# Blank TensorE products first, the first norm's weights through full-height products, and weight tile 1 ahead of token tile 2

## The reference, cut to what matters

```python
def rmsnorm(x, g):
    xf = x.astype(jnp.float32)
    y = xf * lax.rsqrt(jnp.mean(xf * xf, axis=-1, keepdims=True) + EPS)
    return (y * g.astype(jnp.float32)).astype(x.dtype)
...
        hn = rmsnorm(h, mix_pre[l])
...
    u = h @ w_in
    gate_br, x_br = u[..., :D_RNN], u[..., D_RNN:]
```

## Time and profile before

| | us |
|---|---|
| median of three runs | 1112.71 |
| lowest and highest | 1111.16, 1113.22 |
| the profiled execution's own time | 1111.33 |
| its span | 1109.5 |
| TensorE busy in it | 1093.1 |
| first real product starts | 11.77 |

### The profile page before, as it was taken

One profiled execution on the slowest core, in us unless ns is written; L12 is line 12 of the kernel. 1 busy time (PEld: TensorE's weight loads), 2 busy tenths in 40 slices (PEclk: granted clock), 3 DMA queues, 4 the chain that ended last, 5 costly groups with the idle time before them and its releaser, 6 DMA issues.

```text
span 1109.5 us, 17385 instructions
## 1 busy us (share of the span) xinstructions
PE 1093.1 (99%) x6901; PEld 977.4 (88%) x6901; DVE 780.9 (70%) x1117; ACT 557.0 (50%) x980; POOL 14.9 (1%) x34
## 2 busy tenths in 40 slices
PE   8999999999999999999999999999999999999998
PEld 7887787889899999988888888879899999998886
DVE  5788985778688888853347888558788888863334
ACT  6377474555355555532236576545355555542223
POOL 1000000000000000000020000000000000000000
PEclk9999999999999999999999999999999999999999
DMA  6332233234133323333333132122233333333211
GB/s 203 111 91 68 84 98 119 92 90 138 42 111 115 111 85 110 134 116 100 104 80 76 39 97 57 39 76 84 88 115 114 96 95 115 115 133 98 100 50 76
DMA packets 150962, 107.22 MB, mean 97 GB/s; under 512 B 23922, under 2 KB 140770, under 8 KB 150883
## 3 DMA queue, kind: packets, MB, share of 16 engines
q1 hardware_dynamic: 150882, 106.12, 31.7%
HBM read 104.01 MB, written 2.10 MB: 96 GB/s over the span
## 4 chain that ended last, share of the span: by engine, by line
PE 93%; DVE 4%; ACT 2%; DMA 1%; issue 0%; POOL 0%; SPq 0%; DVEq 0%
PE ps L1758 11%; PE ps L1760 11%; PE ps L1762 11%; PE ps L1536 10%; PE ps L1537 10%; PE ps L1540 10%; PE ps L1517 9%; PE ps L1518 8%; PE ps L1519 8%; PE ps L1689 1%; PE ps L1862 1%; PE ps L1889 1%; DVE w_lo L976 1%; DVE work L1166 1%; ACT junk L562 1%; DVE h L1168 1%
## 5 line engine op out<-in xcount | busy, mean ns | idle before, releaser
L976 DVE TENSOR_TENSOR w_lo<-raw,w_hi 128x1024 fp32r<-128x1024 f32 x113 | 140.4, 1245 | 166.5 <-ACT w_hi L558 166.3
L558 ACT CAST w_hi<-raw 128x1024 fp32r<-128x1024 f32 x114 | 118.9, 1046 | 168.9 <-PE ps L1540 147.5
L1517 PE MATMUL ps<-x_hi,w_hi 128*128 128x512 f32 (+1 forms) x520 | 180.8, 348 | 4.9 <-DVE w_lo L976 4.2
L1518 PE MATMUL ps<-x_lo,w_hi 128*128 128x512 f32 (+1 forms) x520 | 177.5, 341 | 0.0
L1519 PE MATMUL ps<-x_hi,w_lo 128*128 128x512 f32 (+1 forms) x520 | 177.4, 341 | 0.0
L1758 PE MATMUL ps<-t_hi,w_hi 128*128 128x256 f32 x576 | 163.5, 284 | 0.2
L1760 PE MATMUL ps<-t_lo,w_hi 128*128 128x256 f32 x576 | 163.4, 284 | 0.0
L1762 PE MATMUL ps<-t_hi,w_lo 128*128 128x256 f32 x576 | 163.4, 284 | 0.0
L1536 PE MATMUL ps<-w_hi,t_hi 128*128 128x512 f32 x352 | 137.3, 390 | 0.0
L1537 PE MATMUL ps<-w_lo,t_hi 128*128 128x512 f32 x352 | 137.3, 390 | 0.0
L1762 PE MATMUL ps<-x_hi,w_lo 128*128 128x256 f32 x432 | 122.5, 284 | 0.0
(11 more groups left out here) (202 smaller groups left out, 2011.0 us busy)
## 6 DMA issues: line engine op xcount, KB each, us to landing
raw<-in_ffn_w_gu SPq DMA_DIRECT2D x88, 512.0 KB, 4.0
raw<-in_ffn_w_down SPq DMA_DIRECT2D x44, 512.0 KB, 3.3
raw<-in_a_w_in SPq DMA_DIRECT2D x24, 512.0 KB, 4.3
raw<-in_a_w_out SPq DMA_DIRECT2D x12, 512.0 KB, 3.5
raw<-in_b_w_q SPq DMA_DIRECT2D x16, 256.0 KB, 3.4
raw<-in_b_w_o SPq DMA_DIRECT2D x16, 256.0 KB, 3.8
h<-in_x SPq DMA_DIRECT2D x4, 512.0 KB, 5.8
result<-h SPq DMA_DIRECT2D x3, 512.0 KB, 2.6
```

The lines of the kernel that those rows point to most:

```text
L558: nc.scalar.copy(w_hi[:, t % 4, :], raw[:, t % 4, :]).then_inc(w_hi_ready, 1)
L976: v.tensor_tensor(w_lo[:, t % 4, :], raw[:, t % 4, :], w_hi[:, t % 4, :].bitcast(F32), ALU.subtract)\
L1517: nc.tensor.matmul(out_ps, hi_w, hi_x, start=first, stop=False)
L1518: nc.tensor.matmul(out_ps, hi_w, lo_x, start=False, stop=False)
```

## The change

Five edits, all at the start of the kernel:

- VectorE first of all zeroes `gain_rows` (128 partitions by 1,024 float32) and `blank` (128 by 512 bf16) and fills `ones` (128 by 128 float32) with ones. GpSimd no longer fills the row of ones.
- SP loads x0 first, then waits until `gain_rows` is zeroed, and loads the row of weights into its first partition; the rest follows in the order of before.
- TensorE waits for the three fills, makes four bf16 products of 128 x 128 by 512 columns of zeros into PSUM bank 5, then spreads the weights by products of full height (the rows but the first are zero), and makes four more blank products.
- TensorE multiplies weight tile 1 with the first 256 tokens directly behind tile 0, and turns token tile 2 only then, followed by token tile 3.
- ScalarE splits weight tile 1 before it squares x2, and tile 2 before the high part of token tile 2; VectorE makes the low parts of tiles 1 and 2 one step earlier likewise.

```diff
--- before.py
+++ after.py
@@ -151,7 +151,6 @@
     ri_raw = sb("ri_raw", [P, 2, RI_COLS], F32, at["gpost"])
     junk = sb("junk", [P, D], BF16)
     ident = sb("ident", [P, P])
-    ones_row = sb("ones_row", [1, P])
     eps = sb("eps", [P, 1])
     ss = sb("ss", [P, 32])
     std = sb("std", [P, 33])
@@ -186,7 +185,9 @@
     r_rows = sb("r_rows", [P, P], F32, at["e_u"])
     dist_i = sb("dist_i", [P, WIN], I32, at["e_u"] + 4 * P)
     dist_n = sb("dist_n", [P, WIN], F32, at["e_u"] + 8 * P)
-    gain_row = sb("gain_row", [1, D], F32, at["y_lo"])
+    gain_rows = sb("gain_rows", [P, D], F32, at["y_lo"])
+    ones = sb("ones", [P, P], F32, at["y_lo"] + 4 * D)
+    blank = sb("blank", [P, S], BF16, at["y_hi"])
 
 
     at["top"] = U
@@ -286,6 +287,8 @@
         xhi_ready = sem("xhi_ready")
         xlo_ready = sem("xlo_ready")
         eps_ready = sem("eps_ready")
+        blank_ready = sem("blank_ready")
+        gain_blank = sem("gain_blank")
         xf_ready = sem("xf_ready")
         t_ready = sem("t_ready")
         thi_ready = sem("thi_ready")
@@ -433,8 +436,9 @@
             def load_x(c):
                 sp.dma_start(h[:, c, :], x[0, c * P:(c + 1) * P, :]).then_inc(x_landed[c], 16)
 
-            sp.dma_start(gain_row[:, :], mix_pre[0:1, :]).then_inc(gain_landed, 16)
             load_x(0)
+            sp.wait_ge(gain_blank, 1)
+            sp.dma_start(gain_rows[0:1, :], mix_pre[0:1, :]).then_inc(gain_landed, 16)
             load_x(1)
             load_in(0)
             load_x(2)
@@ -505,7 +509,6 @@
                 pool.wait_ge(pool_steps, steps.inc(ins))
 
             nc.gpsimd.memset(eps[:, :], EPS).then_inc(eps_ready, 1)
-            nc.gpsimd.memset(ones_row[:, :], 1.0)
             then(nc.gpsimd.memset(ident[:, :], 0.0))
             nc.gpsimd.affine_select(out=ident[:, :], in_=ident[:, :], compare_op=ALU.not_equal, fill=1.0, base=0,
                                     pattern=[[-1, P]], channel_multiplier=1).then_inc(ident_ready, 1)
@@ -588,11 +591,11 @@
             split_hi(0)
             for i in range(4):
                 first_high(i)
+            split_hi(1)
             square_x(2)
-            split_hi(1)
             square_x(3)
+            split_hi(2)
             first_high(4)
-            split_hi(2)
             first_high(5)
             act.wait_ge(lam_abs, 1)
             nc.scalar.activation(sp_t[:, 1, :], sp_t[:, 0, :], ACT.Exp, scale=-1.0).then_inc(lam_exp, 1)
@@ -1007,15 +1010,18 @@
                 v.tensor_tensor(x_lo[:, k0:k1, tok], turned_in(t)[:, k0:k1, :], x_hi[:, k0:k1, tok].bitcast(F32),
                                 ALU.subtract).then_inc(first_lo, 1)
 
+            v.memset(gain_rows[:, :], 0.0).then_inc(gain_blank, 1)
+            v.memset(blank[:, :], 0.0)
+            v.memset(ones[:, :], 1.0).then_inc(blank_ready, 1)
             for i in range(4):
                 normalise_x(i)
             for i in range(4):
                 first_low(i)
+            split_lo(1)
             normalise_x(4)
-            split_lo(1)
             normalise_x(5)
+            split_lo(2)
             first_low(4)
-            split_lo(2)
             first_low(5)
 
 
@@ -1629,12 +1635,20 @@
                     token_half(b, 2, t, 1)
 
 
+            def busy(n):
+
+                for _ in range(n):
+                    nc.tensor.matmul(bank(5), blank[:, 0:P], blank[:, :], start=True, stop=True)
+
+            pe.wait_ge(blank_ready, 1)
+            busy(4)
             pe.wait_ge(ident_ready, 1)
             pe.wait_ge(gain_landed, 16)
             for half in range(2):
-                ins = nc.tensor.matmul(bank(6 + half), ones_row[:, :], gain_row[:, half * S:half * S + S], start=True,
+                ins = nc.tensor.matmul(bank(6 + half), ones[:, :], gain_rows[:, half * S:half * S + S], start=True,
                                        stop=True)
             ins.then_inc(gain_spread, 1)
+            busy(4)
 
             def first_turn(i):
                 t, k0, k1 = START_PARTS[i]
@@ -1652,8 +1666,8 @@
             for i in range(4):
                 first_turn(i)
             first_half(0)
+            first_half(1)
             first_turn(4)
-            first_half(1)
             first_turn(5)
             first_half(2)
             pe.wait_ge(params_landed, 16 * 8)
```

## The result

Twenty runs of the changed kernel have a median of 1114.99 us (1112.52 to 1115.71); twenty of the kernel before, 1112.51 (1111.08 to 1114.17). The ratio is 1.0017, 95% interval 1.0011 to 1.0023: slower by about 2 us, clear of no change, and 1 us above the top of the range forecast. The profiled execution took 1115.27 us against 1111.33. Both kernels' runs lie in groups a microsecond or more apart: the lowest runs differ by 1.4 us, the medians by 2.5.

The account below looks back on a forecast made before the run. TensorE, busy 99%, bounds the kernel, so the first real product's start decides. +0.95 - 0.25 = +0.7 on the profiled 1111.33 gave 1112.0; half the spread, 0.4, made it 1112.4, range 1110.7 to 1114.0.

Parts of the forecast that it names:

- T0: Start of TensorE's first real product, 11.77 us before; forecast 12.7, a later start moving the whole rest of the kernel.
- (a): VectorE's three memsets ahead of everything: 1.9 us in all, blanks starting at 2.65, no cost to VectorE.
- (b): SP's queue: x0 0.41 us earlier, later loads behind a wait; tile 0 lands at 8.0, x1 at worst 7.0.
- the weight chain: Tile 0's load, ScalarE's rounding, GpSimd's low part, ending at 11.65 before; forecast to allow T0 likely at 11.6.
- (c) to (e): Gain row lands at 4.5, four blanks take 1.9 us, full-height gain products 3.1, ending at 7.6.
- (f): VectorE's first normalising product waits for the gain products until 7.6; with 5.12 us behind it, T0 12.7, +0.95.
- (g): The swap of tile 1's first half and token tile 2's turn: no turn waits afterwards, -0.25 us.
- The term that was put at nothing: TensorE's clock behind T0: already risen by then in the profiled run, so blanks can give back nothing there.
- half of the spread above the profiled run: Median over profiled execution: blanks take away what a late-rising clock causes, so only half stands, 0.4 us.
- the slower one (the row queues): SP's gain row lands at 6.6 behind x0, the clock stays low, T0 16.1, time 1115.4; chance 0.06.
- Rival 4: The swap stalls: tile 1 lands over a us after 12.15, its first half waits, 1113 us; chance 0.11.
- Rival 3: Blanks don't raise TensorE's clock: gain products take 3.75 us, T0 14.0, time 1113.3; chance 0.12.

Follow-up runs that it names:

- row_second: The kernel before with x0 loaded ahead of the row of weights, without a wait: lowest +2.2, median +2.0 us, ratio 1.0019.
- swap_only: The kernel before with only tile 1's first half put ahead of the turn of token tile 2: lowest -0.25, median +0.15 us, ratio 0.9996.
- act_queue: The changed kernel with the row of weights and its wait moved from SP's to ScalarE's queue: lowest +2.8, median +2.0 us, ratio 1.0025.
- row_waits: The kernel before with x0 ahead of the row and SP waiting between them on a VectorE memset: lowest +3.25, median +2.2 us, ratio 1.0023.
- wait_only: The kernel before, row still first, with SP waiting on a VectorE memset between x0 and x1: lowest +0.8, median +0.9 us, ratio 1.0009.
- two_fills: The kernel before with the swap and blanks only where TensorE idles, three behind the gain products, two behind the last turn: ratio 0.9991, again 0.9994.
- early_fill: The kernel `two_fills` with two more blanks ahead of the gain products: 1111.20 us against 1112.64 for the kernel before, ratio 0.9991.

## Why the prediction was wrong

The forecast was "about the same". The sum gave the start +0.7 us where the profiled execution lost 2.5: 0.3 of the difference lies in T0, 1.5 behind it. Point by point:

- (a) The memsets took 0.91, 0.27 and 0.17, less than the 1.9 in all; VectorE started at 1.01 and not at 0.73, so the blanks began at 2.40 for 2.65. Right.
- (b) **This is the step that failed** ahead of T0. It said that the loads queue for bandwidth anyway, that x1 lands at worst at 7.0 and tile 0 at worst at 8.85, likely 8.0. x1 came at 7.97, tile 0, 6.7 us behind its issue, at 9.41. The bounds took the time from issue to landing from one execution, in which SP never paused. For x1 the pause and the row make it longer: 4.4 to 4.7 us with the row first or on another queue, 5.3 with the wait, 5.4 with the row, 5.1 to 6.5 with both. For tile 0 the bound was too narrow even without them: it took 5.6 to 7.3 us in kernels with the row first and no pause. So both chains were late, the weight chain too, and T0 was 13.06 for 12.7.
- (c) to (e) Row at 4.66 for 4.5, blanks 1.89 for 1.9, gain products 2.94 for 3.1, their end 7.60 for 7.6: right here, near the lucky end of a term that gave 2.60 to 3.75 in other executions. In the other two profiles of this kernel it gave 3.75 and 3.70, so that the gain's own chain, and not x1, held T0 at 13.29 and 13.49.
- (f) 5.12 from the gain's end to T0 was right where x1 is not late (`row_second`: 5.23). Here it was 5.46.
- (g) -0.25 was right (`swap_only`, lowest -0.25); the turns stand back to back and no gap opened behind T0.
- **The term that was put at nothing**, and the larger one where it comes, is the clock behind T0. The prediction asked what blanks win in clock, and saw nothing behind T0 to lose it again: between the turns and the first real product TensorE idles 1.26 us, twice the 0.64 of before, and in the profiled execution the clock fell at 13.5 for 3.4 us, 1.5 us lost, as in about three of ten executions. Its reason, that the clock had risen by T0 in the profiled run, says nothing of a fall. The same step let half of the spread above the profiled run go as a win of the blanks, 0.4 us; instead the median moved from 1.4 to 2.5 us above the lowest run.

By this the loss adds up, as an estimate: 1.3 to 1.7 us at T0, 0.25 back by the swap, 0.4 to 0.6 of the fall on average, together 1.5 to 2.1 where the ratio means 1.9.

Of the rivals, the slower one (the row queues) did not come: the row landed at 4.66, not 6.6; `act_queue`, where it landed at 6.28, has T0 at 14.75 and not 16.1. Rival 4's condition came true, tile 1 landed at 13.5 for 12.15, but no product waited for it. Rival 3's 3.75 us of gain products came in one profile, with the clock up behind them. The true loss is a mixture that none of the four priced.

The rule that transposes do not bring the full clock (the Trainium skill, "TensorE: Matmul & The Clock Gate", part 4) was set aside with reason: in `row_second`, whose only full-height work ahead of T0 is transposes, sixteen take 3.55 us from 9.50 and the real products from 13.81 run at full speed, which the rule would not give. But `row_waits` and `wait_only` have the same transposes, and their first products run at 1.2 GHz for 3.3 to 3.6 us, as the rule would have it. So here transposes were followed by the full clock in some executions and not in others.

## What to carry to other kernels

Take the first transfers of a kernel as one stream: a wait put into it, or a small row moved behind a large tile, costs more than its length (0.4 us of pause brought x1 1.0 us late in `wait_only`), and the tiles behind it pay. Before adding work that warms an engine's clock, look at what stands between it and the dense stretch: a lighter stretch there can give the clock back, so fill gaps, and delay nothing for it. Where runs fall in groups, compare lowest runs and medians, sort the single runs by their recorded clock, and use one profile only for the stretch that the change touches.

## What the runs showed that was not expected

- 4 KB issued on a second, empty queue at 1.96 us landed at 6.28; behind 512 KB on the first queue it landed by 4.3 to 4.9, and ahead of everything by 2.25.
- With a pause of 0.85 us in SP's stream and the row behind it, the DMA engines moved 216 to 253 GB/s from 4 to 8 us in three executions of the changed kernel, at a busy share of 0.8; 365 to 373 in the kernels with the row first and no pause.
- Products one row high, 3.75 us of them with full-height blanks around them, left TensorE at 1.2 GHz until after 10 us; at full height, with the same blanks ahead, the clock rose in or right behind them.
- With four or five instructions on TensorE more than the changed kernel has, one instruction of VectorE, 570 us later, took 0.9 to 1.1 us longer, in three profiles of three; five or seven more than the kernel before has (`two_fills`, `early_fill`) did not do it.
- Tile 0 took 5.6 to 7.3 us from issue to landing in five executions whose loads are issued in the same order at the same times.
